# Turning the input of a streaming encoder: the RMS norm taken after the transpose instead of before it

## The chip, the cores and the metric

One core of a Trainium2 chip runs the whole program. The metric is device time in microseconds (us) of one execution. The engines are PE (TensorE, matrix products and transposes), DVE (VectorE), ACT (ScalarE), POOL (GpSimd) and SP (SyncE, which only issues DMAs here). All data are float32.

## The reference, cut to what matters

Two layers of a hybrid encoder are evaluated for 1024 prompt tokens and 32 sample tokens that share all weights. What matters here is the very first step, the RMS norm of the input of layer 0:

```python
def rms_norm(x, g):
    xf = x.astype(jnp.float32)
    y = xf * lax.rsqrt(jnp.mean(xf * xf, axis=-1, keepdims=True) + EPS)
    return (y * g.astype(jnp.float32)).astype(x.dtype)
...
        hp = rms_norm(yp, norm_g[l])
        hs = rms_norm(ys, norm_g[l])
```

`yp` is 1024 x 1024 and `ys` is 32 x 1024. Later the un-normed input is needed again for the residual sum.

## The kernel before

The program runs stage after stage, and each stage ends in a barrier of all engines: `turn_input`, then `gdn` (layer 0's delta-rule mixer), `band` (its chunk-band attention), `finish_layer` (output projection and memory attention), then `gla` and a second `finish_layer` for layer 1. The diff touches only the first stage, `turn_input`.

`turn_input` reads the input in 9 tiles of tokens: 8 tiles of 128 prompt tokens and a last one with the 32 sample tokens (`rows(t)`). In memory a token is a row of D = 1024 numbers; the later matrix products want features on the partitions. The stage makes two such turned copies, each with KD = 8 blocks of 128 features: `xT` (the raw input, a buffer called `x_kept` outside, which the trace shows under that name) and `hT` (the normed input times the gain `g`). Both are in SBUF, 128 partitions by 8 by 1152.

Each tile goes through the engines like this:

- SP issues one load per tile (L116), then the first four weight loads of the next stage (`load_ahead`, L59).
- ACT squares the tile with tokens on partitions and sums the squares on the way (L161, which makes a second small instruction that reads the accumulator), takes the logarithm (L163) and the exponential of minus half of it (L165). That is one number per token, `rs`, a column of 128 partitions by 1.
- DVE multiplies the tile by that column into `xN` (L193).
- PE turns the raw tile in 8 transposes of 128 x 128 into PSUM (`TX`, L139), and one tile behind turns `xN` in 8 transposes into `TH` (L126, `normed`).
- `TX` is copied to `xT` by ACT (L154, `turned`) for seven tiles and by DVE for tiles 2 and 5 (L198, `BY_DVE`).
- DVE multiplies `TH` by the gain into `hT` (L182, `out`).
- POOL only makes the identity (L172, L174) and is free after that.

Every buffer between engines has two halves, and each engine runs its own fixed list of instructions with semaphore waits. The next stage begins on PE with the products of L512 (`hT` and the weights `Wb`); its lists begin once every engine has passed the barrier.

Of the kernel before, what the change touches and what calls it, by code (L numbers as in the profile page):

```python
# [6 lines left out]
F32 = mybir.dt.float32  # L7
# [78 lines left out]
def turn_input(nc, ident, ones, eps, x_in, xT, gain, hT, ahead):  # L86

    with ExitStack() as ctx:
# [6 lines left out]
        xN = sb("xN", [128, 2, D])  # L95
        sq = sb("sq", [128, D])
        ss, rs = sb("ss", [128, TILES]), sb("rs", [128, TILES])
        g = sb("g", [128, KD])
        TX = ctx.enter_context(nc.psum_tensor("turn_TX", [128, 2, KD, 128], F32))
        TH = ctx.enter_context(nc.psum_tensor("turn_TH", [128, 2, KD, 128], F32))  # L100
        g_ld, x_ld = sem("g_ld"), [sem(f"x_ld{t}") for t in range(TILES)]
        cleared, ident_ok, consts = sem("cleared"), sem("ident_ok"), sem("consts")
        squared, rooted, rs_ok, scaled = sem("squared"), sem("rooted"), sem("rs_ok"), sem("scaled")
        x_turned, h_turned, x_act, x_dve, h_out = (sem("x_turned"), sem("h_turned"), sem("x_act"), sem("x_dve"), sem("h_out"))
        BY_DVE = (2, 5)
        by_dve = [len([t for t in BY_DVE if t < n]) for n in range(TILES + 1)]

# [3 lines left out]
        with nc.Block() as block:  # L111
# [8 lines left out]
            def _(pe):  # L120
                def normed(t):
                    r = rows(t)
                    pe.wait_ge(scaled, t + 1)
                    wait(pe, h_out, t - 1)
                    for k in range(KD):
                        mm = pe.transpose(TH[:, t % 2, k, 0:r], xN[0:r, t % 2, 128 * k:128 * k + 128], ident[0:r, 0:r])  # L126
                    mm.then_inc(h_turned, 1)

                pe.wait_ge(ident_ok, 1)
                for t in range(TILES):  # L130
                    r = rows(t)
                    pe.wait_ge(x_ld[t], 16)
                    if t >= 2:
                        if t - 2 in BY_DVE:
                            pe.wait_ge(x_dve, by_dve[t - 1])
                        else:
                            pe.wait_ge(x_act, t - 1 - by_dve[t - 1])
                    for k in range(KD):
                        mm = pe.transpose(TX[:, t % 2, k, 0:r], xS[0:r, t, 128 * k:128 * k + 128], ident[0:r, 0:r])  # L139
                    mm.then_inc(x_turned, 1)  # L140
                    if t:
                        normed(t - 1)
                normed(TILES - 1)

            @block.scalar
            def _(act):
# [3 lines left out]
                def turned(t):  # L150
                    if t in BY_DVE:
                        return
# [3032 lines left out]
```

## Time and profile before

| | us |
|---|---|
| median of 3 runs | 3585.02 (3584.09 to 3587.85) |
| the profiled execution, its own time | 3584.09 |
| its span in the trace | 3582.4 |
| PE busy over the span | 3484.0 (97%) |
| DVE, ACT, POOL busy | 1173.9, 1102.7, 512.4 |
| last instruction of `turn_input` ends | 26.63 after the span's start |
| first product of the next stage starts | 27.50 |

The span runs from the first to the last instruction in the trace. PE is the engine that is nearly always busy; a stage's end matters for the total when PE has nothing to do until the next stage starts.

### The profile page before, as it was taken

The page shows a single profiled execution, that of the slowest core. Times are in us where ns is not written, and L with a number is a line of the kernel's source. Part 1 is how long each engine was busy: PE and PEld are TensorE (multiplying, and loading weights), DVE is VectorE, ACT ScalarE, POOL GpSimd, SP SyncE. Part 2 cuts the span into 40 slices and gives each one's busy share as a digit, 9 for nine tenths or more (in the row PEclk, how much of TensorE's full clock was granted, in tenths as well). Part 3 has the DMA queues.
Part 4 walks back from the last instruction along what each step waited for, and adds up shares of the span by engine and source line. Part 5 has one row for each costly group of instructions (what it writes and reads, how often), then busy time and mean ns, then how long its engine had stood idle before and what let it go on. Part 6 is the DMA issues. An engine that isn't in the chain of part 4 may idle for free. (4 is left out here: it accounts for less than half of the span.)

```text
span 3582.4 us, 47127 instructions
## 1 busy us (share of the span) xinstructions
PE 3484.0 (97%) x16559; PEld 2563.4 (72%) x16559; DVE 1173.9 (33%) x2941; ACT 1102.7 (31%) x2810; POOL 512.4 (14%) x518
## 2 busy tenths in 40 slices
PE   9999999999799999999999998999999999899999
PEld 5777777776477778777766675677777777566676
DVE  3555555555133323333320233022222122220223
ACT  4343433333234333334210342122223222210242
POOL 2345543453000000000000002000000000011000
PEclk9999999999899999999999999999999999999999
DMA  6212411103322332212260102111111111371101
GB/s 161 52 32 38 37 36 27 37 24 116 72 40 42 46 41 43 42 29 92 92 213 30 36 24 74 36 30 45 39 50 44 44 30 33 117 232 48 35 1 49
DMA packets 246000, 206.64 MB, mean 58 GB/s; under 512 B 19903, under 2 KB 222943, under 8 KB 245831
## 3 DMA queue, kind: packets, MB, share of 16 engines
q1 hardware_dynamic: 239902, 194.16, 22.3%
q10 hardware_dynamic: 5936, 10.34, 0.8%
q8 instruction: 99, 1.62, 0.2%
q14 instruction: 63, 0.52, 0.0%
HBM read 158.49 MB, written 45.99 MB: 57 GB/s over the span
## 5 line engine op out<-in xcount | busy, mean ns | idle before, releaser
L512 PE MATMUL gdn_pj<-hT,Wb 128*128 128x352 f32 x1536 | 513.3, 460 | 1.6 <-PEq L45 1.6
L2014 PE MATMUL gla_pj<-hT,Wb 128*128 128x352 f32 x1536 | 471.7, 461 | 6.9 <-PEq L45 6.2
L1464 PE MATMUL band_pj<-hT,Wb 128*128 128x384 f32 (+1 forms) x1152 | 390.8, 468 | 25.4 <-PEq L45 14.4
L2014 PEld LDWEIGHTS gla_pj<-hT,Wb 128*128 128x128 f32 x1536 | 290.8, 190 | 157.2 <-issue 9.1
L512 PEld LDWEIGHTS gdn_pj<-hT,Wb 128*128 128x128 f32 x1536 | 264.8, 191 | 89.3 <-issue 1.7
L1464 PEld LDWEIGHTS band_pj<-hT,Wb 128*128 128x128 f32 x1152 | 208.8, 194 | 110.1 <-issue 30.9
L2010 PE MATMUL gla_pj<-gla_Wv,hT 128*128 128x256 f32 (+1 forms) x1152 | 266.8, 381 | 0.0
L2010 PEld LDWEIGHTS gla_pj<-gla_Wv,hT 128*128 128x128 f32 x1152 | 217.2, 190 | 31.8
L1649 ACT ACTIVATE band_E<-band_NS,band_nm 128x576 f32<-128x576 f32 (+9 forms) x136 | 89.8, 660 | 215.8 <-DVE band_nm L1727 215.4
L1226 POOL TENSOR_TENSOR x_kept<-gdn_AT,gdn_level 128x384 f32<-128x384 f32 x144 | 144.3, 1033 | 35.7 <-DVE gdn_TT L1008 18.5
L1494 PE MATMUL band_pj<-Wb,hT 128*128 128x128 f32 x1152 | 144.2, 275 | 0.0
L1557 PEld LDWEIGHTS band_PX<-band_ET,band_VT 128*128 128x128 f32 x976 | 127.0, 192 | 20.3
L1494 PEld LDWEIGHTS band_pj<-Wb,hT 128*128 128x128 f32 x1152 | 136.5, 192 | 0.7
L1727 DVE CUSTOM_DVE_ANT_0 band_NS<-band_SC,band_bias 128x576 f32<-128x576 f32 (+9 forms) x136 | 83.2, 612 | 153.1 <-issue 152.2
L1557 PE MATMUL band_PX<-band_ET,band_VT 128*128 128x128 f32 x976 | 131.0, 275 | 0.0
L2729 PE MATMUL fin_ps<-fin_R,fin_Wx 128*128 128x384 f32 (+1 forms) x384 | 124.7, 468 | 2.2 <-DVE fin_xT L3020 2.1
L2720 PE MATMUL fin_ps<-hT,Wb 128*128 128x384 f32 (+1 forms) x384 | 125.9, 463 | 0.0
L1659 ACT ACTIVATE band_ET<-band_PT 128x512 f32<-128x512 f32 (+3 forms) x136 | 70.7, 520 | 158.3 <-PE band_PX L1537 89.6
L1527 PE MATMUL band_SC<-band_KN,band_Qz 128*128 128x288 f32 (+3 forms) x448 | 115.8, 375 | 3.6 <-issue 3.6
L2693 PE MATMUL fin_ps<-hT,fin_Wq 128*128 128x384 f32 (+1 forms) x384 | 117.2, 459 | 0.0
L2661 PE MATMUL fin_ps<-hT,Wb 128*128 128x384 f32 (+1 forms) x384 | 115.9, 459 | 0.0
L2983 DVE TENSOR_TENSOR fin_xT<-fin_xT,fin_ps 128x384 f32<-128x384 f32 (+1 forms) x48 | 24.7, 520 | 274.4 <-PE fin_ps L2661 241.7
(413 smaller groups left out, 5375.4 us busy)
## 6 DMA issues: line engine op xcount, KB each, us to landing
Wb<-in_l_w_in_dram SPq DMA_DIRECT2D x96, 512.0 KB, 6.6
fin_xT<-x_features SPq DMA_DIRECT2D x16, 528.0 KB, 7.6
fin_R<-o_features SPq DMA_DIRECT2D x16, 528.0 KB, 9.4
Wb<-in_l_w_mkv_dram SPq DMA_DIRECT2D x8, 1024.0 KB, 5.4
Wb<-in_l_w_out_dram SPq DMA_DIRECT2D x16, 512.0 KB, 3.7
gla_Wv<-in_l_w_in_dram SPq DMA_DIRECT2D x8, 1024.0 KB, 5.5
o_features<-gla_OF ACTq DMA_DIRECT2D x14, 528.0 KB, 5.7
gdn_GB<-gate_rows SPq DMA_DIRECT2D x8, 544.0 KB, 3.6
```

What stands on the lines that cost most here:

```text
L512: mm = pe.matmul(pj[:, m % 2, 0:w], W[:, j, k, :], hT[:, k, c0:c0 + w], start=k == 0, stop=k == KD - 1)
L1226: pool.tensor_tensor(g3(BT, g), g3(AT, g), mask, ALU.mult).then_inc(masked, 1)
L1464: mm = pe.matmul(out[:, 0:w], W[:, BAND_SLOT[j], k, :], hT[:, k, c0:c0 + w], start=k == 0, stop=k == KD - 1)
L1494: mm = pe.matmul(out[:, 0:128], hT[:, k, 128 * i:128 * i + 128], W[:, BAND_SLOT[3], k, :], start=k == 0, stop=k == KD - 1)
L1527: mm = pe.matmul(out[:, b, 0:w], q, KN[p][:, k0 + w * b:k0 + w * b + w], start=True, stop=True)
L1557: mm = pe.matmul(PX[:, 1, :], v, ET[:, u % 2, 128 * b:128 * b + 128], start=b == 0, stop=b == blocks(u) - 1)
L2010: mm = pe.matmul(pj[:, m % 2, 0:wv], hT[:, k, 128 * x:128 * x + 128], Wv[:, k, 0:wv], start=k == 0, stop=k == KD - 1)
L2014: mm = pe.matmul(pj[:, m % 2, 0:w], W[:, SLOT[kind], k, :], hT[:, k, c0:c0 + w], start=k == 0, stop=k == KD - 1)
L2661: mm = pe.matmul(ps[:, 3 * (n % 2) + c, 0:w], weights, src[:, c0:c0 + w], start=i == 0, stop=i == len(tiles) - 1)
L2693: mm = pe.matmul(ps[:, i % 3, 0:w], Wqt[:, h, k, :], hT[:, k, c0:c0 + w], start=k == 0, stop=k == KD - 1)
L2720: mm = pe.matmul(out[:, 0:w], Wz[:, x, k, :], hT[:, k, c0:c0 + w], start=k == 0, stop=k == KD - 1)
L2729: mm = pe.matmul(out[:, 0:w], Wo[:, k, 128 * x:128 * x + 128], O[:, k, c0:c0 + w], start=k == 0, stop=k == M_H - 1)
```

## The change

The norm is now taken with features on the partitions. Only the raw tile is turned (`TP`, two halves, L139 now), and ACT copies every tile to `xT`. POOL squares the turned tile from `xT` into `sq`. PE sums the squares over all 1024 features by 8 products with a 128 x 128 matrix of ones, so that every partition of `PS` holds the sums of all tokens of the tile. ACT takes logarithm and exponential of that, now 128 partitions by 128 tokens instead of one column. DVE multiplies `xT` by the gain (a column) and by `rs` (a full tile) in 8 instructions per tile, one per block of features, into `hT`. The transposes of `xN`, the scaling into `xN`, DVE's two copies and ACT's squares are gone.

```diff
             def _(pe):
+                def total(t):
+                    pe.wait_ge(squared, t + 1)
+                    wait(pe, rooted, t - 1)
                     for k in range(KD):
-                        mm = pe.transpose(TH[:, t % 2, k, 0:r], xN[0:r, t % 2, 128 * k:128 * k + 128], ident[0:r, 0:r])
-                    mm.then_inc(h_turned, 1)
+                        mm = pe.matmul(PS[:, t % 2, 0:rows(t)], ones[:, :], sq[:, t % 2, k, 0:rows(t)], start=k == 0, stop=k == KD - 1)
+                    mm.then_inc(summed, 1)
...
                 for t in range(TILES):
                     r = rows(t)
                     pe.wait_ge(x_ld[t], 16)
+                    wait(pe, copied, t - 1)
                     for k in range(KD):
+                        mm = pe.transpose(TP[:, t % 2, k, 0:r], xS[0:r, t, 128 * k:128 * k + 128], ident[0:r, 0:r])
+                    mm.then_inc(turned, 1)
                     if t:
+                        total(t - 1)
+                total(TILES - 1)
...
             def _(act):
+                def root(t):
+                    r = rows(t)
+                    act.wait_ge(summed, t + 1)
+                    wait(act, h_out, t - 1)
+                    act.activation(rs[:, t % 2, 0:r], PS[:, t % 2, 0:r], ACT.Ln, scale=1.0 / D, bias=eps[:, 0:1]).then_inc(rooted, 1)
+                    act.wait_ge(rooted, t + 1)
+                    act.activation(rs[:, t % 2, 0:r], rs[:, t % 2, 0:r], ACT.Exp, scale=-0.5).then_inc(rs_ok, 1)
...
                 for t in range(TILES):
                     r = rows(t)
-                    act.activation(sq[0:r, :], xS[0:r, t, :], ACT.Square, accum_out=ss[0:r, t:t + 1]).then_inc(squared, 1)
+                    act.wait_ge(turned, t + 1)
+                    act.activation(xT[:, :, cols(t)], TP[:, t % 2, :, 0:r], ACT.Copy).then_inc(copied, 1)
                     if t:
+                        root(t - 1)
+                root(TILES - 1)
...
             def _(pool):
+                for t in range(TILES):
+                    pool.wait_ge(copied, t + 1)
+                    wait(pool, summed, t - 1)
+                    pool.tensor_tensor(sq[:, t % 2, :, 0:rows(t)], xT[:, :, cols(t)], xT[:, :, cols(t)], ALU.mult).then_inc(squared, 1)
...
             def _(dve):
                 for t in range(TILES):
                     r = rows(t)
+                    dve.wait_ge(copied, t + 1)
                     dve.wait_ge(rs_ok, t + 1)
-                    dve.tensor_scalar(xN[0:r, t % 2, :], xS[0:r, t, :], rs[0:r, t:t + 1], None, ALU.mult).then_inc(scaled, 1)
+                    for k in range(KD):
+                        mm = dve.scalar_tensor_tensor(hT[:, k, cols(t)], xT[:, k, cols(t)], g[:, k:k + 1], rs[:, t % 2, 0:r],
+                                                      ALU.mult, ALU.mult)
+                    mm.then_inc(h_out, 1)
```

In the helper `wait`, a wait for a count of zero or less is left out. So ACT may start the root of tile t once tiles 0 to t-2 are in `hT`, and PE may turn tile t once tiles 0 to t-2 are copied.

## Rows read from the trace of the kernel before

**Rows 1.** The page's first part: busy time, share and instructions per engine.

```profile
PE 3484.0 (97%) x16559; PEld 2563.4 (72%) x16559; DVE 1173.9 (33%) x2941; ACT 1102.7 (31%) x2810; POOL 512.4 (14%) x518
```

**Rows 2.** Windows: stretch, length, then busy us (count) per engine, granted clock, DMA share, GB/s.

```profile
0.00:26.63 26.63, 18.67 (x144) 16.57 (x144) 19.07 (x23) 21.05 (x44) 0.70 (x6) 1.00 0.96 218
27.50:60.00 32.50, 32.50 (x127) 16.45 (x128) 0.96 (x4) 6.18 (x9) 8.28 (x32) 1.00 0.81 220
```

**Rows 3.** Timeline of PE in `turn_input`: start, length, line, shape, count, idle before.

```profile
4.88 4.04 PE L139 MATMUL turn_TX<-ident,turn_xS 128*128 128x128 f32 x16 [4.88 <-DMA turn_xS<-in_x_prompt_dram]
...
10.60 1.04 PE L126 MATMUL turn_TH<-ident,turn_xN 128*128 128x128 f32 x8
...
27.50 14.44 PE L512 MATMUL gdn_pj<-hT,Wb 128*128 128x352 f32 x48 [1.60 <-PEq L45]
```

**Rows 4.** Timeline of DVE at the end of `turn_input`.

```profile
23.20 1.22 DVE L182 TENSOR_TENSOR hT<-turn_TH,turn_g 128x1024 f32<-128x1024 f32 x1
24.42 0.74 DVE L193 TENSOR_SCALAR turn_xN<-turn_xS,turn_rs 32x1024 f32<-32x1024 f32 x1
25.09 1.54 DVE L182 TENSOR_TENSOR hT<-turn_TH,turn_g 128x1024 f32<-128x1024 f32 x2
```

**Rows 5.** Timeline of ACT: one tile in `turn_input`.

```profile
16.08 1.05 ACT L161 ACTIVATE turn_sq<-turn_xS 128x1024 f32<-128x1024 f32 x1
...
17.68 1.01 ACT L154 ACTIVATE x_kept<-turn_TX 128x1024 f32<-128x1024 f32 x1
```

**Rows 6.** Groups by line and shape, ACT: busy us, mean ns of one, idle before.

```profile
L2843 ACT ACTIVATE fin_rs<-fin_ps,eps 128x384 f32<-128x384 f32 x4 | 2.2, 562 | 0.0
L845 ACT ACTIVATE x_kept<-x_kept 128x128 f32<-128x128 f32 x64 | 19.1, 298 | 0.1
```

**Rows 7.** Groups by line and shape, POOL.

```profile
L1191 POOL TENSOR_TENSOR gdn_conv<-gdn_conv,gdn_tap 128x1091 f32<-128x1091 f32 x24 | 50.7, 2113 | 1.9
L3088 POOL TENSOR_TENSOR fin_acc<-fin_acc,fin_sq 128x384 f32<-128x384 f32 x28 | 27.9, 996 | 462.6 <-ACT fin_sq L2837 462.6
L1211 POOL TENSOR_TENSOR gdn_WQ<-gdn_act,gdn_EG 128x384 f32<-128x384 f32 x24 | 23.4, 1003 | 0.0
L3088 POOL TENSOR_TENSOR fin_acc<-fin_acc,fin_sq 128x288 f32<-128x288 f32 x14 | 11.1, 794 | 65.1 <-ACT fin_sq L2837 65.0
L2361 POOL COPY gla_Ss<-gla_sall 128x256 f32 x6 | 2.3, 390 | 0.0
```

**Rows 8.** Groups by line and shape, DVE.

```profile
L2966 DVE SCALAR_TENSOR_TENSOR hT<-fin_xT,fin_g,fin_rs 128x384 f32<-128x384 f32 x32 | 17.3, 613 | 6.6 <-ACT fin_rs L2845 6.6
L1706 DVE SCALAR_TENSOR_TENSOR band_Qz<-band_raw,band_g,band_rs 64x32 f32<-64x32 f32 x16 | 3.9, 245 | 0.0
```

**Rows 9.** Timeline of DVE: nine instructions of 128 columns without a pause.

```profile
100.66 2.45 DVE L937 SCALAR_TENSOR_TENSOR x_kept<-gdn_GB,gdn_gn,gdn_causal 128x128 f32<-128x128 f32 x9
```

**Rows 10.** Timeline, 123.50 to 126.2 us: DVE and POOL beside each other.

```profile
123.50 0.55 DVE L1008 TENSOR_TENSOR gdn_TT<-ident,x_kept 128x384 f32<-128x384 f32 x1
...
123.72 1.19 POOL L1226 TENSOR_TENSOR x_kept<-gdn_AT,gdn_level 128x384 f32<-128x384 f32 x1 [2.49 <-DVE gdn_TT L1008]
123.97 1.36 DVE L1008 TENSOR_TENSOR gdn_TT<-ident,x_kept 128x384 f32<-128x384 f32 x1
...
124.87 1.31 POOL L1226 TENSOR_TENSOR x_kept<-gdn_AT,gdn_level 128x384 f32<-128x384 f32 x1
```

**Rows 11.** Timeline, 214.5 to 217.2 us: DVE and POOL beside each other.

```profile
214.59 1.84 DVE L977 SCALAR_TENSOR_TENSOR gdn_conv<-gdn_U,gdn_cwc,gdn_conv 128x1091 f32<-128x1091 f32 x1
...
214.46 0.83 POOL L1206 TENSOR_TENSOR x_kept<-x_kept,gdn_cur 128x384 f32<-128x384 f32 x1 [11.18 <-ACT x_kept L799]
...
215.61 1.51 POOL L1206 TENSOR_TENSOR x_kept<-x_kept,gdn_cur 128x384 f32<-128x384 f32 x1 [0.33 <-ACT x_kept L799]
```

**Rows 12.** One line of the kernel each: shortest, median, longest ns, first and last start.

```profile
L977 DVE SCALAR_TENSOR_TENSOR gdn_conv<-gdn_U,gdn_cwc,gdn_conv x48: 1354/1356/1845, 104.6 to 816.5; 128x1091 f32<-128x1091 f32 x48
L1021 DVE TENSOR_TENSOR gdn_TT<-gdn_TT,gdn_X x120: 514/517/555, 129.5 to 859.8; 128x384 f32<-128x384 f32 x120
```

More of the change, by code:

```diff
@@ L94, in turn_input @@
         xS = sb("xS", [128, TILES, D])
-        xN = sb("xN", [128, 2, D])
-        sq = sb("sq", [128, D])
-        ss, rs = sb("ss", [128, TILES]), sb("rs", [128, TILES])
+        sq = sb("sq", [128, 2, KD, 128])
+        rs = sb("rs", [128, 2, 128])
         g = sb("g", [128, KD])
-        TX = ctx.enter_context(nc.psum_tensor("turn_TX", [128, 2, KD, 128], F32))
-        TH = ctx.enter_context(nc.psum_tensor("turn_TH", [128, 2, KD, 128], F32))
+        TP = ctx.enter_context(nc.psum_tensor("turn_TP", [128, 2, KD, 128], F32))
+        PS = ctx.enter_context(nc.psum_tensor("turn_PS", [128, 2, 512], F32))
         g_ld, x_ld = sem("g_ld"), [sem(f"x_ld{t}") for t in range(TILES)]
         cleared, ident_ok, consts = sem("cleared"), sem("ident_ok"), sem("consts")
[L103 to L106, printed above, removed]
+        turned, copied, squared, summed, rooted, rs_ok, h_out = (sem("turned"), sem("copied"), sem("squared"), sem("summed"),
+                                                                 sem("rooted"), sem("rs_ok"), sem("h_out"))
         def cols(t):
@@ L148, in _ @@
                 act.preload_act_table_set("natural_log_exp_and_others")
-                def turned(t):
-                    if t in BY_DVE:
-                        return
-                    act.wait_ge(x_turned, t + 1)
-                    act.activation(xT[:, :, cols(t)], TX[:, t % 2, :, 0:rows(t)], ACT.Copy).then_inc(x_act, 1)
+                def root(t):
[5 more added lines that the diff above has]
+                    act.activation(rs[:, t % 2, 0:r], rs[:, t % 2, 0:r], ACT.Exp, scale=-0.5).then_inc(rs_ok, 1)
                 act.wait_ge(consts, 1)
@@ L158, in _ @@
                     r = rows(t)
-                    act.wait_ge(x_ld[t], 16)
-                    wait(act, squared, t)
-                    act.activation(sq[0:r, :], xS[0:r, t, :], ACT.Square, accum_out=ss[0:r, t:t + 1]).then_inc(squared, 1)
-                    act.wait_ge(squared, t + 1)
-                    act.activation(rs[0:r, t:t + 1], ss[0:r, t:t + 1], ACT.Ln, scale=1.0 / D, bias=eps[0:r, 0:1]).then_inc(rooted, 1)
-                    act.wait_ge(rooted, t + 1)
-                    act.activation(rs[0:r, t:t + 1], rs[0:r, t:t + 1], ACT.Exp, scale=-0.5).then_inc(rs_ok, 1)
+                    act.wait_ge(turned, t + 1)
+                    act.activation(xT[:, :, cols(t)], TP[:, t % 2, :, 0:r], ACT.Copy).then_inc(copied, 1)
                     if t:
-                        turned(t - 1)
-                turned(TILES - 1)
+                        root(t - 1)
+                root(TILES - 1)
             @block.gpsimd
```

28 lines of the change are left out of this document (2 added, 26 removed).

## The prediction

> **What bounds the kernel now.** I read the page's engine shares first, then windows of the first stage and of the stretch behind it, then the timelines of PE, DVE and ACT in the stage, and last the groups and timelines that price what the change adds. PE is busy 97% of the span [rows 1]. In the first 26.63 us it is busy for only 18.67 us, and from 27.50 on it is busy without a gap, at a granted clock of 1.00 [rows 2]. So the stage's end sets the total: whatever the stage grows or shrinks by, the rest of the program is pushed or pulled by, since every engine waits at the barrier between 26.63 and 27.50 [rows 3, 4]. An earlier or later start changes nothing in what follows it, as no wait on a DMA shows on PE there that could take up a delay. Inside the stage no engine is full: ACT needs 16.08 to 18.69, 2.61 us, for a tile that it also copies [rows 5], PE needs 1.04 us for a group of 8 transposes, twice a tile [rows 3], and DVE's last gain product ends the stage at 25.09 + 1.54 = 26.63 [rows 4].
>
> **What the change takes and gives, part by part.**
>
> ACT loses the square, its accumulator read and two tiny instructions. It gains a logarithm and an exponential of 128 columns. The nearest rows are 0.562 us for a logarithm of 384 columns out of PSUM and 0.298 us for 128 columns out of SBUF [rows 6]; the larger shape less 256 columns at about 0.8 ns (0.298 us for 128 against 1.01 for the 1024 of a copy, over 896 [rows 5, 6]) gives some 0.36. With 0.31 for the exponential, the root costs 0.67, call it 0.7 with the semaphore between. A tile then costs ACT 0.7 + 1.01 = 1.7 us instead of 2.6. This saving is real, but ACT's time is no longer what the stage waits for.
>
> PE swaps 8 transposes for 8 products with the same 128 columns: 1.04 us each way [rows 3], call it 1.1 until the result is seen. No gain. The first 16 transposes took 4.04 us where 8 later ones take 1.04, so the first two tiles will again take 2.0 each.
>
> DVE loses per tile a scale of 0.74 and a gain product of 1.22 us [rows 4], and the two copies. It gains 8 instructions of 128 columns with two SBUF inputs. The same form ran nine times in 2.45 us, 0.26 apart [rows 9]; the same operation into `hT` at 384 columns takes 0.613 [rows 8]. Eight cost 7 x 0.26 + 0.35 = 2.2 us. So DVE is slower per tile, 2.2 against 1.96 us. The last tile of 32 columns pays 8 times nearly the same fixed cost: 0.245 each [rows 8], about 0.16 apart if they overlap as the long ones do, 1.4 us.
>
> POOL gains a product of 128 x 1024 per tile. No row has this size. Two tensor inputs cost 0.996 us for 384 columns and 0.794 for 288, so 2.1 ns a column, and in three pieces of 128 it is 1.003 [rows 7]: 0.996 + 640 x 0.0021 = 2.35, and 2.4 with the eight pieces. From below, 2.113 us for 1091 columns in one piece gives 2.0; from above, 8/3 of 1.003 gives 2.7. I take 2.4, because the operands lie in pieces as in the 1.003 row. The last tile, 256 columns, costs 0.75.
>
> The DVE and POOL parts cannot be laid side by side. At 123.97 a DVE product with two SBUF inputs took 1.36 us where the one before took 0.55: it ended only after POOL's product, which had begun at 123.72. POOL's next one took 1.31 instead of 1.00 behind it [rows 10, 7]. The form that the change uses (tensor, column, tensor, all in SBUF) did the same: 1.84 us beside POOL against a median of 1.356, and POOL's product then took 1.51 against 0.83 [rows 11, 12]. A DVE product with one input in PSUM keeps to 514 to 555 ns over 120 times, with POOL busy beside many of them [rows 12]. So a two-SBUF-input instruction of DVE and a product of POOL take turns, one whole instruction each. Before the change POOL had nothing to do in this stage, and now every DVE instruction of it meets one.
>
> The Trainium skill (SBUF — State Buffer, "Who interferes with whom") states the rule that speaks against this change: a DVE instruction with two SBUF inputs shares its second read interface with GpSimd, and whichever issues first blocks the other for a whole instruction. The rows above agree, and by it the sum below stands; by its absence the sum would be that of the second case.
>
> **The sum.** Tile 0 is turned at 4.88 + 2.0 = 6.9, copied at 7.9, squared at 10.3, summed at 11.4, its root ready at 12.1. PE's list has the sums of tile 0 ahead of turning tile 2, so that is turned at 12.4 and copied at 13.4. POOL squares tile 1 until 12.7 and tile 2 from 13.4 to 15.8; DVE gets in three instructions before and one between; tile 3 is copied at 15.8 and squared until about 18.5; DVE's other four put tile 0 into `hT` at about 19.6. From there ACT's two-deep wait makes a loop: `hT` of tile t, then the root of t+2 (0.7), the copy of t+4 (1.0), its square on POOL (2.4, after the DVE instruction then running, 0.1), then what is left of DVE's eight for tile t+1, of which six or seven ran during root and copy (0.3 to 0.4). That is 4.5 us a tile, which is also the sum of the two engines' work, 2.2 + 2.4, less a little. Four turns bring tile 4 to 19.6 + 18.0 = 37.6. POOL's big squares are then done. Tiles 5, 6, 7 take 2.2 each plus 0.8 for POOL's last small square, and tile 8 takes 1.4: 7.4 + 1.4 = 8.8, end at 46.4. Against 26.63 this is +19.8 us. The profiled execution has 3584.1, which is 0.9 under the median of the runs shown; 3585.0 + 19.8 = 3604.8, and as some 0.1 us of each recorded duration seems not to block the other (the DVE instruction at 123.97 ended at 125.33, where 124.91 + 0.55 would be 125.46 [rows 10]), I take 3604.
>
> Bounds inside this case: POOL at 2.0 makes the loop 4.1 and the end 43.5 (3602), at 2.7 it makes 4.8 to 4.9 and the end 49 (3608). DVE's 0.26 might be 0.23 or 0.30: two us either way.
>
> **The rivals.**
>
> Second case, no collision worth the name: DVE and POOL run side by side. Then two tiles go round in transposes 1.0 + copy 1.0 + square 2.4 + sums 1.1 = 5.5 us, because PE and ACT each take the turned tile t+2 only after the sums and root of t. Turned tiles 2, 4, 6, 8 at 12.4, 17.9, 23.4, 28.6; the last root at 31.6, DVE done with tile 7 at 33.3 and tile 8 at 34.7. That is +8.1: 3593, with POOL at 2.0 3591 and at 2.7 3595. Rows 10 and 11 speak against it; for it speaks only that 128-column instructions are shorter than those seen to collide.
>
> Third case, on the other side, not slower: POOL's price. If a product of a tensor with itself costs POOL what a one-input copy does, 0.390 for 256 columns [rows 7], some 1.0 for 1024, and it slips between DVE's instructions, DVE is the bound. Its first instruction can start at 6.9 + 1.0 + 1.0 + 1.1 + 0.7 = 10.7, and 8 x 2.2 + 1.4 = 19.0 more end at 29.7: +3, 3588, within 0.2%. It needs a square under about 1.7 us; all two-tensor rows say over 2.0. Even this is not faster than before, because DVE's work alone, begun at 10.7, ends later than 26.63 unless its instructions come under 0.22 us apart.
>
> Fourth case, the clock: PE would be busy about 2.1 of each 4.5 us. A group of 8 took 2.0 us at the start of the trace and 1.04 later [rows 3], which is what half the clock would do. In the loop PE's groups are not on the path (tile t+4 is turned while DVE works), so the price is one group at the end, 1 us, and the first products of the next stage: they come 48 in 14.44 us, 0.3 each [rows 3], and ten of them at half the clock would lose 3 us. 3604 + 4 = 3608.
>
> The Trainium skill (TensorE: Matmul & The Clock Gate, "HAM oscillation — how this bites in real kernels") says that waits between short groups of products can throw PE back to its lower clock. The trace grants 1.00 through this stage before the change, with PE busy 70% of it, and no row of this stage shows the fall.
>
> **How the numbers follow.** Taking turns as summed: 0.70. With the lower clock on top: 0.07. No collision: 0.14. The cheap square: 0.05. The remaining 0.04 is for anything else, a gain included. The range 3593 to 3609 holds the first two and part of the second case; the likeliest case's own range is 3600 to 3608. A change under 0.2%, 7.2 us, is about what a measurement of this kernel can't tell from none. The second case straddles that line, two parts in three above it. Slower by more than 0.2%: 0.70 + 0.07 + 0.09 + 0.01 = 0.87. Within: 0.05 + 0.05 + 0.01 = 0.11. Faster: 0.02.
>
> **What would show it.** The stage's last DVE instruction ends near 46, and PE starts the next stage 0.9 us later. POOL's squares last 2.4 us, a little more where they wait for DVE, with gaps of some 2 us between them from tile 4 on. DVE's instructions are mostly 0.35 long, but one or two in each eight last over 2 us, each over one of POOL's. If instead none of DVE's is over 0.5 us, the second case holds. Copies of tiles 4 to 7 on ACT start 4.5 us apart. Everything from the barrier on is as before, only later. The prediction is wrong if POOL squares in under 1.7 us, if DVE's short instructions slip through, or if something behind the barrier takes the delay back.

## The result, and the profile after

The change makes the kernel slower: 3609.3 us (median of 4 runs, 3608.6 to 3609.8) against 3586.4 (4 runs, 3584.1 to 3590.2), a ratio of 1.0063, 95% interval 1.0048 to 1.0079. That is 22.9 us more, where 17.6 were forecast (3604 less the 3586.4 of these runs) and 3609 was the upper end of the range. The profiled execution took 3610.3 us, 26.2 more than that of before.

The page's first part after the change, to be laid beside [rows 1]:

```profile
PE 3499.8 (97%) x16631; PEld 2577.4 (71%) x16631; DVE 1178.3 (33%) x2993; ACT 1095.7 (30%) x2794; POOL 533.1 (15%) x527
```

PE has 72 more instructions and is busy for 15.8 us more; DVE has 52 more. Both counts turn out to matter. So does a line of the page's third part: packets, MB and share of the queue q14, whose kind the profile gives as `instruction`, before and after.

```profile
q14 instruction: 63, 0.52, 0.0%
q14 instruction: 87, 0.71, 0.1%
```

Windows of the kernel after (columns as in [rows 2]): the whole stage, the first 48 products of the next, and three stretches chosen for the clock column, third from the end.

```profile
0.00:48.31 48.31, 33.54 (x216) 31.65 (x216) 26.14 (x75) 15.56 (x28) 21.25 (x15) 0.89 0.62 134
49.17:66.58 17.41, 17.41 (x49) 10.61 (x50) 0.62 (x3) 2.37 (x4) 7.90 (x30) 0.83 0.69 209
30.00:35.00 5.00, 0.00 (x0) 0.00 (x0) 3.69 (x15) 1.20 (x2) 5.00 (x1) 0.97 0.16 40
35.00:40.00 5.00, 4.51 (x24) 4.28 (x24) 0.00 (x0) 0.65 (x2) 2.29 (x2) 0.50 0.00 0
50.60:52.00 1.40, 1.40 (x4) 0.88 (x3) 0.00 (x0) 0.00 (x0) 1.36 (x7) 0.50 0.23 14
```

The stage ends at 48.31 instead of 26.63. The timeline of DVE, its rows in the stage from the first product on; the last line is one instruction out of the first row:

```profile
14.45 19.24 DVE L182 SCALAR_TENSOR_TENSOR hT<-x_kept,turn_g,turn_rs 128x128 f32<-128x128 f32 x48 [12.54 <-ACT turn_rs L149]
40.13 2.55 DVE L182 SCALAR_TENSOR_TENSOR hT<-x_kept,turn_g,turn_rs 128x128 f32<-128x128 f32 x8 [6.44 <-ACT turn_rs L149]
44.83 3.49 DVE L182 SCALAR_TENSOR_TENSOR hT<-x_kept,turn_g,turn_rs 128x128 f32<-128x128 f32 x16 [2.15 <-ACT turn_rs L149]
...
22.20 1.98 DVE L182 SCALAR_TENSOR_TENSOR hT<-x_kept,turn_g,turn_rs 128x128 f32<-128x128 f32 x1
```

The timeline of POOL, the squares of tiles 4, 5 and 6:

```profile
21.98 2.05 POOL L169 TENSOR_TENSOR turn_sq<-x_kept 128x1024 f32<-128x1024 f32 x1 [1.43 <-ACT x_kept L155]
24.67 2.05 POOL L169 TENSOR_TENSOR turn_sq<-x_kept 128x1024 f32<-128x1024 f32 x1 [0.64 <-ACT x_kept L155]
29.18 6.26 POOL L169 TENSOR_TENSOR turn_sq<-x_kept 128x1024 f32<-128x1024 f32 x1 [2.47 <-ACT x_kept L155]
```

Laid over each other, these rows show two kinds of waiting. POOL's square of tile 4 began at 21.98, and the DVE instruction issued at 22.20 took 1.98 us instead of 0.34, ending 0.15 behind the square. The same happened beside the squares at 15.95, 18.61 and 24.67. At 29.18 it went the other way: DVE was inside a row of products without a pause (48 from 14.45 to 33.69), and POOL's square lasted 6.26 us where the others take 1.89 to 2.05. It ended 1.75 us behind DVE's row, so it did its work only when that row was over, some 4.4 us late.

The timeline of PE: the first group of transposes, the first sums (of tile 0), later sums, and the groups around that square:

```profile
4.67 1.94 PE L132 MATMUL turn_TP<-ident,turn_xS 128*128 128x128 f32 x8 [4.67 <-DMA turn_xS<-in_x_prompt_dram]
...
9.77 3.79 PE L122 MATMUL turn_PS<-turn_sq,ones 128*128 128x128 f32 x16 [0.69 <-POOL turn_sq L169]
...
17.92 2.05 PE L122 MATMUL turn_PS<-turn_sq,ones 128*128 128x128 f32 x16 [0.45 <-POOL turn_sq L169]
...
28.66 1.04 PE L132 MATMUL turn_TP<-ident,turn_xS 128*128 128x128 f32 x8
35.49 3.78 PE L122 MATMUL turn_PS<-turn_sq,ones 128*128 128x128 f32 x16 [5.80 <-POOL turn_sq L169]
...
49.17 17.41 PE L497 MATMUL gdn_pj<-hT,Wb 128*128 128x352 f32 x48 [2.97 <-PEq L45]
66.51 14.53 PE L682 MATMUL gdn_P<-hT,gdn_wab 128*40 128x512 f32 x48
```

The 8 products of a sum are recorded as 16 passes and take 2.05 us (the row at 17.92), against 1.04 for 8 transposes. PE sat idle for 5.80 us before the sums of tile 6, which then took 3.78: the granted clock was 0.97 while it waited and 0.50, the lower level of 1.2 GHz, from 35 on (windows above). The next stage starts at 49.17 against 27.50 [rows 3], 21.7 late, and its first 48 products take 17.41 us instead of 14.44: the clock is 0.50 again at 50.60. At 66.51 PE is 24.6 us late.

Behind that the delay does not stay what it is. Start of the same PE work, after less before, from the two timelines (an "end" is the last product of L512 for `gdn` and of L1464 for `band`, after the change L497 and L1449):

| work | us late |
|---|---|
| first products of the stage `gdn` | 21.7 |
| `gdn_P` (66.51 against 41.87) | 24.6 |
| end of `gdn` (843.8 against 807.1) | 36.7 |
| start of `band` | 35.8 |
| end of `band` (1710.2 against 1686.5) | 23.7 |
| `gla` | 22.3 |
| last `fin`, its second group of products | 27.9 |
| end of the span | 26.2 |

The list of waits after the change has two rows that are not in that of before (waiting engine and tile, what it waited for, total us, times, longest):

```profile
DVE gdn_cwc L937 <- issue: 12.9, 5, 2.7
DVE gdn_cz L943 <- issue: 8.9, 5, 2.0
```

and that of before has one that is not in the one of after:

```profile
PE band_pj L1464 <- issue: 8.0, 2, 5.8
```

### The profile page after: what moved, and what is told of

It is laid out like the page before. It is cut to its first block and busy times, and to the rows that moved or that the text cites. A ratio compares the mean times of both kernels' runs of the same rounds, so it can differ in the third digit from the quotient of the medians.

```text
span 3608.6 us, 47321 instructions
## 1 busy us (share of the span) xinstructions
PE 3499.8 (97%) x16631; PEld 2577.4 (71%) x16631; DVE 1178.3 (33%) x2993; ACT 1095.7 (30%) x2794; POOL 533.1 (15%) x527
## 3 DMA queue, kind: packets, MB, share of 16 engines
q8 instruction: 100, 1.64, 0.2%
## 5 line engine op out<-in xcount | busy, mean ns | idle before, releaser
L497 PE MATMUL gdn_pj<-hT,Wb 128*128 128x352 f32 x1536 | 516.3, 462 | 3.0 <-PEq L45 3.0
L1449 PE MATMUL band_pj<-hT,Wb 128*128 128x384 f32 (+1 forms) x1152 | 387.1, 465 | 16.8 <-PEq L45 13.8
L497 PEld LDWEIGHTS gdn_pj<-hT,Wb 128*128 128x128 f32 x1536 | 266.3, 192 | 92.1 <-issue 5.5
L1449 PEld LDWEIGHTS band_pj<-hT,Wb 128*128 128x128 f32 x1152 | 207.2, 192 | 99.7 <-issue 19.5
L1995 PEld LDWEIGHTS gla_pj<-gla_Wv,hT 128*128 128x128 f32 x1152 | 217.2, 190 | 31.8
L1211 POOL TENSOR_TENSOR x_kept<-gdn_AT,gdn_level 128x384 f32<-128x384 f32 x144 | 144.2, 1032 | 35.8 <-DVE gdn_TT L993 18.5
L2705 PE MATMUL fin_ps<-hT,Wb 128*128 128x384 f32 (+1 forms) x384 | 124.8, 460 | 0.0
L3073 POOL TENSOR_TENSOR fin_acc<-fin_acc,fin_sq 128x384 f32<-128x384 f32 (+1 forms) x42 | 39.0, 929 | 532.2 <-ACT fin_sq L2822 532.0
L2354 POOL TENSOR_TENSOR gla_OR<-gla_OR,gla_rs 128x768 f32<-128x768 f32 x24 | 35.3, 1469 | 552.4 <-ACT gla_rs L2196 552.4
```

The costliest lines, as they stand in the source:

```text
L497: mm = pe.matmul(pj[:, m % 2, 0:w], W[:, j, k, :], hT[:, k, c0:c0 + w], start=k == 0, stop=k == KD - 1)
L1211: pool.tensor_tensor(g3(BT, g), g3(AT, g), mask, ALU.mult).then_inc(masked, 1)
L1449: mm = pe.matmul(out[:, 0:w], W[:, BAND_SLOT[j], k, :], hT[:, k, c0:c0 + w], start=k == 0, stop=k == KD - 1)
L1995: mm = pe.matmul(pj[:, m % 2, 0:wv], hT[:, k, 128 * x:128 * x + 128], Wv[:, k, 0:wv], start=k == 0, stop=k == KD - 1)
L2705: mm = pe.matmul(out[:, 0:w], Wz[:, x, k, :], hT[:, k, c0:c0 + w], start=k == 0, stop=k == KD - 1)
```

## The experiments

All times are medians against runs of the kernel before on the same chip (medians 3587.3 to 3587.6). "Late" is the start of the first `gdn` products less 27.50.

**e1: no shared read.** The change with the root in PSUM, so that DVE's product reads one SBUF tensor only.

```diff
-        rs = sb("rs", [128, 2, 128])
+        rs = ctx.enter_context(nc.psum_tensor("turn_rs", [128, 2, 512], F32))
```

> The changed kernel with one edit: the tile rs that ACT writes and DVE reads lies in PSUM instead of SBUF. All arithmetic is as in the changed kernel. Theory (DVE and POOL take turns because DVE's instructions have two SBUF inputs): now no DVE instruction lasts over 0.5 us, where nine lasted 0.7 to 2 us, and no square of POOL lasts over 2.0 us, where one lasted 6.26. The loop of turning 1.04, copying 1.02, squaring 1.9 and summing 1.95 us then sets the pace, 6.0 us for two tiles, PE never idles for 5 us, its clock stays up, and the stage ends near 38 instead of 48.3; the next stage's first 48 products take 14.4 us again. Total 11 to 13 us over the kernel before, 3597 to 3599. Rival (the two engines only look coupled, the waits come from the semaphores or from any SBUF traffic): DVE's long instructions and the end near 48 stay, total 3609.

3601.2 us (5 runs), ratio 1.0037 (1.0023 to 1.0051): 8 us less than the change. DVE ends the stage at 39.10 instead of 48.31, late 12.5. One line each of e1's kernel (shortest, median, longest ns):

```profile
L182 DVE SCALAR_TENSOR_TENSOR hT<-x_kept,turn_g,turn_rs x72: 242/342/349, 14.3 to 38.9; 128x128 f32<-128x128 f32 x64, 128x32 f32<-128x32 f32 x8
L169 POOL TENSOR_TENSOR turn_sq<-x_kept x9: 613/1892/1893, 7.8 to 33.4; 128x1024 f32<-128x1024 f32 x8, 128x256 f32<-128x256 f32 x1
```

and the same line of the change:

```profile
L182 DVE SCALAR_TENSOR_TENSOR hT<-x_kept,turn_g,turn_rs x72: 244/340/1984, 14.4 to 48.1; 128x128 f32<-128x128 f32 x64, 128x32 f32<-128x32 f32 x8
```

The median is the same, the longest fell from 1984 ns to 349, and no square lasts over 1893. One operand moved out of SBUF removes both kinds of waiting, so they hang on DVE's second SBUF input and not on the semaphores. That is worth 9.2 us at the stage's end, and 3.9 of these are the clock's, as e2 shows. What is left, 12.5 us late with no collision at all, is the second case of the prediction, which had put its end at 34.7.

**e2: PE kept busy.** The change with 48 transposes of the identity between the turning of tile 7 and the sums of tile 6, where PE had been idle.

```diff
+                    if t == 7:
+                        for _ in range(48):
+                            pe.transpose(PJ[:, 0:128], ident[:, :], ident[:, :])
                     if t:
                         total(t - 1)
```

> The changed kernel with one addition: after turning tile 7 PE does 48 more transposes of the identity into a spare PSUM bank, some 5.3 us of work in a stretch where it idled 5.8 us. Theory (a granted clock of 0.50 from about 35 to 54 us cost 4 us in the stage and 3 us in the 48 products behind the barrier): the clock stays at 1.00, the sums of tile 6 take 1.95 instead of 3.8 us, the stage ends near 44.4 instead of 48.3, the first 48 products of the next stage take 14.4 instead of 17.4, total about 7 us less than the changed kernel, 3602. POOL's square of 6.26 us stays. Rival (the clock did not matter, DVE or POOL set the end): the end stays within 1 us of 48.3.

PE's timeline in e2:

```profile
29.18 5.40 PE L137 MATMUL turn_PJ<-ident 128*128 128x128 f32 x48
35.40 2.05 PE L123 MATMUL turn_PS<-turn_sq,ones 128*128 128x128 f32 x16 [0.82 <-POOL turn_sq L173]
```

POOL's square still lasts 6.26, but the sums behind it take 2.05 instead of 3.78, and DVE ends at 44.38 instead of 48.31. So of the stage's growth 3.9 us came from the clock, and its fall inside the stage from PE's idle time. At the barrier it falls again (3.48 us idle, first 48 products 17.18). The kernel's time did not follow the stage: 3611.6 us (4 runs), ratio 1.0065 (1.0048 to 1.0082). Its `band` takes back only 6.3 us where that of the change takes back 12.1: a wait of PE for nothing that the profile shows is back there, of 5.0 us. The table below comes to that.

**e3: DVE lets POOL go first.** The change with DVE's products of tile 4 waiting until tile 6 is squared.

```diff
                     dve.wait_ge(rs_ok, t + 1)
+                    if t == 4:
+                        dve.wait_ge(squared, 7)
```

> The changed kernel with one wait more: DVE starts tile 4 only when POOL has squared tile 6. Theory (POOL's square of tile 6, ready at 29.18, got no turn until DVE's unbroken row of instructions ended at 33.7, and PE's idle time and slower clock come from that): the square of tile 6 takes under 2.3 us and ends near 31.2 instead of 35.4, the clock stays at 1.00, the stage ends near 44 or earlier, total 7 to 10 us under the changed kernel, 3599 to 3602. Rival (the square was long for another reason): it still takes over 5 us. Second rival (the total of both engines' work sets the end whatever the order): the end moves by less than 1 us.

POOL's timeline in e3:

```profile
22.53 5.30 POOL L169 TENSOR_TENSOR turn_sq<-x_kept 128x1024 f32<-128x1024 f32 x2 [1.91 <-ACT x_kept L155]
30.05 1.89 POOL L169 TENSOR_TENSOR turn_sq<-x_kept 128x1024 f32<-128x1024 f32 x1 [2.22 <-ACT x_kept L155]
...
37.06 5.62 POOL L169 TENSOR_TENSOR turn_sq<-x_kept 128x256 f32<-128x256 f32 x1 [2.35 <-ACT x_kept L155]
```

The square of tile 6, at 30.05, is down to 1.89. But that of tile 4 now takes 3.40 of the first row's 5.30: it was kept out for 1.5 us and then got in at 24.1, between two instructions of a row of DVE that went on. And the small last one, 0.71 us in the change, takes 5.62: POOL is kept out for 4.9 us there instead. DVE's row around it ends at 42.21, 0.47 before the square:

```profile
32.08 10.13 DVE L184 SCALAR_TENSOR_TENSOR hT<-x_kept,turn_g,turn_rs 128x128 f32<-128x128 f32 x32 [2.52 <-POOL turn_sq L169]
```

The stage is as late as ever (21.8), and the time is 3609.2 us (4 runs), ratio 1.0057 (1.0041 to 1.0074). The long square is thus no property of tile 6; any square that meets a long row of DVE can be kept out.

**e4: another phase.** A memset of 128 x 64 (0.15 us) on POOL ahead of the square of tile 6, so that it asks at another point of DVE's row.

```diff
+                    if t == 6:
+                        pool.memset(late[:, :], 0.0)
                     pool.tensor_tensor(sq[:, t % 2, :, 0:rows(t)], xT[:, :, cols(t)], xT[:, :, cols(t)], ALU.mult).then_inc(squared, 1)
```

> The changed kernel with one addition: POOL clears a spare 128 x 64 tile, 0.14 us, between its waits and the square of tile 6, so that the square asks for its turn 0.1 to 0.2 us later within DVE's beat of 0.26 us. Of POOL's squares that began within a row of DVE's, those that began 0.04 to 0.18 us after a DVE instruction got the next turn, and the one that began 0.03 us after lost it for 4.4 us. Theory A (the phase decides): the square of tile 6 now gets the next turn, takes 2.0 to 2.3 us, the clock stays up and the total falls by 7 to 10 us. Theory B (a long row of DVE instructions keeps POOL out, whatever the phase): the square still waits until the row ends and the total stays at 3609.

The first of the two squares in POOL's row at 28.94 again lasts 6.17 us:

```profile
28.84 0.15 POOL L171 MEMSET turn_late<- 128x64 f32 x1 [2.71 <-ACT x_kept L156]
28.94 8.02 POOL L172 TENSOR_TENSOR turn_sq<-x_kept 128x1024 f32<-128x1024 f32 x2
```

3607.6 us (4 runs), ratio 1.0058 (1.0041 to 1.0074), late 21.3. It asked 0.24 us earlier, 0.12 us behind the start of a DVE instruction where that of the change asked 0.03 behind one, and was kept out all the same. Squares that got in at once asked 0.02 to 0.18 us behind one in these two kernels, so an unlucky moment is not the cause.

**e5: no collision and no fall of the clock.** e1 with 26 transposes of the identity behind PE's last sums.

```diff
                 total(TILES - 1)
+                pe.wait_ge(copied, TILES)
+                for _ in range(26):
+                    pe.transpose(TP[:, 0, 0, :], ident[:, :], ident[:, :])
```

> The kernel with rs in PSUM, and after its last sums PE does 26 transposes of the identity into the PSUM that the last copy has freed, some 3 us of work while DVE finishes. In the run with rs in PSUM the granted clock was 0.87 over 35 to 40 us and 0.50 over the next 5, and the first 48 products of the next stage took some 17.1 us instead of 14.44. Theory (the clock fell because PE had next to nothing to do while DVE finished): the clock stays at 1.00 through the barrier and the 48 products take 14.4 to 14.8 us; the stage ends at 39.1 as before, total 2.7 us less than with rs in PSUM alone. Rival (the barrier itself, 1 us without work, lets the clock fall, or the products are slow for another reason): the 48 products stay near 17 us.

PE's timeline in e5:

```profile
35.67 3.04 PE L139 MATMUL turn_TP<-ident 128*128 128x128 f32 x26
39.54 14.44 PE L500 MATMUL gdn_pj<-hT,Wb 128*128 128x352 f32 x48 [0.83 <-PEq L45]
```

The first 48 products take 14.44 us, as before the change, instead of e1's 17.20: 2.8 us of e1's delay were the clock behind the barrier. 3594.8 us (10 runs), ratio 1.0022 (1.0013 to 1.0032). That is 6.4 less than e1; 2.4 more of it come from `band` (table below).

**e6: half the sums.** e1 with the sums over four of the eight blocks.

```diff
-                    for k in range(KD):
+                    for k in range(4):
```

> The kernel with rs in PSUM, with the sums of squares taken over 4 of the 8 blocks of features only (the other 4 are left out). Theory (without collisions two tiles go round in one loop of transposes 1.04, copy 1.02, square 1.89 and sums 1.95 us, so each us of the sums counts once for two tiles): the sums of a tile take 1.0 us, the loop falls from 6.0 to 5.05 us, and the stage ends some 4.5 us earlier, near 34.6. Rival (POOL or DVE sets the pace by itself, their work per tile being 1.89 and 2.2): the end moves by less than 1 us.

DVE ends the stage at 34.42, 4.7 us before e1 does. The loop of two tiles (turning, copy, square, sums) is what sets the stage once the collisions are gone, and PE's sums are on it. The single run took 3609.3 us, though the next stage starts 4.6 us earlier than in e1. Its page counts 16559 instructions of PE, 72 fewer than e1's, and its `band` does not take back the 12 us that e1's does: PE's waits for nothing shown are there as in the kernel before, 7.9 us against 8.0. This was the sign that something behind the stage reacts to the lists of instructions.

**e7: gaps in DVE's row.** The change with a one-column memset behind each of DVE's products but every eighth, 63 in all.

```diff
+                        if k < KD - 1:
+                            dve.memset(gap[:, KD * t + k:KD * t + k + 1], 0.0)
```

> The changed kernel, with DVE clearing one spare column, some 0.06 us without an SBUF input, between the eight instructions of each tile. Theory (POOL is kept out for up to 4.4 us because DVE's row of two-input instructions leaves no gap): each square of POOL gets its turn at the next gap, none lasts over 2.4 us, PE's idle stretch before the sums of tile 6 is gone or under 3 us, and the stage ends at 44 or earlier although DVE has 0.4 us more work per tile. Rival (who gets the turn does not depend on a gap): at least one square still lasts over 3 us.

One line of e7's kernel:

```profile
L170 POOL TENSOR_TENSOR turn_sq<-x_kept x9: 675/1892/1954, 7.9 to 34.9; 128x1024 f32<-128x1024 f32 x8, 128x256 f32<-128x256 f32 x1
```

No square is over 1.95 us, and the stage ends at 42.0 although DVE has 63 instructions more. The one run took 3587.2 us, as fast as the kernel before (3587.5). But the stage is still 15.4 late; the rest was given back elsewhere, and two things had been changed: the gaps and the count.

**e10: the same count, no gaps.** The same 63 memsets in a block ahead of DVE's loop.

```diff
+                for i in range(63):
+                    dve.memset(pad[:, i:i + 1], 0.0)
                 dve.wait_ge(g_ld, 16)
```

> The changed kernel, with 63 clears of a spare column on DVE ahead of the loop, as many as the run with gaps had between its instructions. If the gaps did their work as gaps, the long square of POOL (over 4 us), the idle PE and the end near 48 are back. If the list's length did what remained, DVE's waits in gdn's heads (12.9 and 8.9 us over five heads in the changed kernel) are gone, PE is 24 to 25 us late through all of gdn instead of 36.7 at its end, and the total is near 3597, 12 us under the changed kernel. Rival: the waits in gdn stay and the total is 3609.

POOL's timeline in e10, squares of tiles 6 and 7:

```profile
29.23 8.11 POOL L170 TENSOR_TENSOR turn_sq<-x_kept 128x1024 f32<-128x1024 f32 x2 [2.47 <-ACT x_kept L156]
```

Those 8.11 us for two squares are what the change has too, and the stage ends at 48.35: in e7 it was the gaps that let POOL in. But the time is 3596.1 us (10 runs), ratio 1.0023 (1.0014 to 1.0033), 13 us less than the change, with a stage that is no faster. The count alone gives that.

**e8, e9, e12: the kernel before with padding.** e8 adds 52 one-column memsets to DVE, e9 adds 72 transposes of 32 x 32 to PE, both ahead of the stage's loop, where those engines wait for the first tile; e12 has the 72 and 115 memsets.

```diff
+                for i in range(52):
+                    dve.memset(pad[:, i:i + 1], 0.0)
```
```diff
+                for _ in range(72):
+                    pe.transpose(TX[0:32, 0, 0, 0:32], ident[0:32, 0:32], ident[0:32, 0:32])
```

> The kernel before, with 52 clears of a spare column added on DVE in turn_input while DVE has nothing else to do, so that DVE's list is as much longer as the change made it. Theory (behind the stage the two kernels differ by how their instruction lists lie, not by work: in the changed kernel DVE waits 2.6 us for nothing the profile shows in five heads of gdn and PE runs 12 us later after them, and it runs 12 us earlier again in band): the stage ends at 26.6 us as before, but DVE's waits in gdn's heads appear, and PE is 5 to 12 us later at the end of gdn. Rival (those waits come from the later start of gdn or from what its loads meet): gdn runs as in the kernel before, total within 1.5 us of it.

> The kernel before, with 72 transposes of a 32 x 32 corner of the identity on PE ahead of the first tile, in time in which PE waits for its first load, so that PE's list is as much longer as the change made it. Theory (behind the stage only the place of the instructions in memory differs): the stage ends within 1.5 us of 26.63, gdn runs as before, and PE's two waits in band for which the profile shows no cause, 8.0 us in the kernel before, are gone, so that PE is 8 to 14 us earlier at the end of band and the total is some 8 to 12 us under the kernel before, 3576 to 3580. Rival (band was faster in the changed kernels because it started later, against its loads): total within 2 us of the kernel before.

> The kernel before, with both paddings: 72 small transposes on PE and 115 clears of a spare column on DVE, which is DVE's list at the length of the run with gaps. Theory: the stage ends near 26.6 to 28, no DVE waits in gdn, none of PE's in band, total 8 to 12 us under the kernel before and within 2 us of the run with PE's padding alone, so 3575 to 3580: the shortest of all. Rival: the two paddings disturb each other and the total is at or over the kernel before.

e8: 3598.9 us (9 runs), ratio 1.0033 (1.0022 to 1.0043). e9: 3576.7 (6 runs), 0.9969 (0.9957 to 0.9982). e12: 3575.7 (6 runs), 0.9965 (0.9953 to 0.9977). The stage itself is 0.3, 0.1 and 0.6 late. In e9 and e12 the clock fell behind the barrier all the same: the first 48 products take 16.13 and 15.92 us, with a granted clock of 0.79 and 0.62 from 27 to 30, though PE was idle for 1.6 us there as in the kernel before, where it stayed at 1.00. So the idle time just before the products is not all that decides. e8 has the waits that the change brought, in its own list of waits:

```profile
DVE gdn_cwc L955 <- issue: 12.9, 5, 2.7
DVE gdn_cz L961 <- issue: 8.4, 5, 1.8
PE band_pj L1467 <- issue: 7.7, 1, 7.7
```

The third row is the one of before, and it is missing in e9 and e12. So 52 instructions that do nothing reproduce the change's loss in `gdn`, and 72 others most of its gain in `band` (10.8 of 12.1 us).

**e11: all of it.** e5 with the 63 memsets ahead of the loop.

```diff
+        rs = ctx.enter_context(nc.psum_tensor("turn_rs", [128, 2, 512], F32))
...
+                for _ in range(26):
+                    pe.transpose(TP[:, 0, 0, :], ident[:, :], ident[:, :])
...
+                for i in range(63):
+                    dve.memset(pad[:, i:i + 1], 0.0)
```

> The kernel with rs in PSUM and PE kept busy until the barrier, with the same 63 clears on DVE. Theory: gdn starts 12 us later than in the kernel before and its heads keep that, without DVE's waits; band gives back 12 to 15 us as in the other kernels with the longer PE list; the total is 3583 to 3586, at or a little under the kernel before, from a stage that is 12 us longer. Rival (DVE's waits in gdn come with any later start): total stays at 3595.

3583.1 us (11 runs), ratio 0.9990 (0.9981 to 0.9999), with the stage 12.0 late: 0.1% below the kernel before, hardly told from nothing, and 7.4 us above e12, which has the old stage and the same count on DVE. The changed stage does not pay in any form that was tried.

**The count, over all kernels.** The counts of DVE and PE are from each page's first part; they are of recorded instructions, a product counting twice, a transpose once and a wait for a semaphore not at all. "In `gdn`" is by how much the delay against before grows from `gdn_P` to the end of `gdn`, "in `band`" from the start of `band` to its end, in us.

| kernel | DVE | in `gdn` | PE | in `band` |
|---|---|---|---|---|
| before | 2941 | 0 | 16559 | 0 |
| e9 | 2941 | 0.0 | 16631 | -10.8 |
| e8 | 2993 | +11.5 | 16559 | -3.3 |
| e6 | 2993 | +11.8 | 16559 | -0.4 |
| the change | 2993 | +12.1 | 16631 | -12.1 |
| e1 | 2993 | +11.8 | 16631 | -12.4 |
| e3 | 2993 | +11.8 | 16631 | -12.5 |
| e4 | 2993 | +11.1 | 16631 | -12.3 |
| e5 | 2993 | +11.9 | 16657 | -14.8 |
| e2 | 2993 | +11.6 | 16679 | -6.3 |
| e7 | 3056 | -0.1 | 16631 | -15.1 |
| e10 | 3056 | -0.1 | 16631 | -14.8 |
| e11 | 3056 | -0.1 | 16657 | -14.6 |
| e12 | 3056 | -0.1 | 16631 | -11.4 |

What `gdn` loses goes with DVE's count and with nothing else in the table: 11.1 to 12.1 us in all eight kernels with 2993, 0.1 or less in all with another count. The queue q14 goes with it: 87 or 88 packets and 0.71 or 0.72 MB on the pages of those eight, 63 or 64 packets and 0.52 MB on the pages of the other six. What `band` gives back goes with PE's waits for nothing shown at `band_pj`: 7.7 to 8.0 us of them in the three kernels with 16559, 5.0 in e2, none in the others.

## Why the prediction was wrong in its size

**The step that failed.** "In the loop PE's groups are not on the path", with the lower clock left to a fourth case of 0.07, was the term that put the time outside the range: the clock took 6.9 us by `gdn_P`. Behind it stands a step of the mechanism: "take turns, one whole instruction each", with a square going ahead "after the DVE instruction then running, 0.1". One square waited 4.4 us instead, PE stood idle for it, and the clock fell. Against the 19.8 that were forecast for the profiled run, the stage without the clock's share grew by 17.8 (it would end at 44.4, as e2's does), the clock added 6.9, and the rest of the program, where 12.1 more and 12.1 less cancel, 1.5: 26.2. That the stage's own end came within 1.9 us is luck: it was forecast 2.0 too late and lost 3.9 to the clock.

**What held.** The stage's end sets the time up to the barrier; the change is slower; a DVE instruction with two SBUF inputs and a square of POOL block each other, and e1 shows that this costs 9.2 us at the stage's end with what the clock adds to it. The two-tile loop is what remains without it. The next stage starts 0.86 us behind the last DVE instruction, as forecast.

**The likeliest case's end, 46.4 forecast, 48.31 measured.** The sum came near by terms that missed in both directions.

- POOL's square was taken at 2.4 and measures 1.89 (2.05 with a DVE instruction beside it). No price for operands "in pieces" shows; even the bound from below, 2.0, was too high. All its rows were of two different tensors or of other shapes.
- PE's sums, "8 products with the same 128 columns: 1.04 us each way", measure 1.95 to 2.05. A product is recorded as two passes, a transpose as one. "No gain" was a loss of 0.9 us a tile. This term is on the loop of the second case: 34.7 forecast, 39.1 measured in e1. Two tiles go round in 1.0 + 1.0 + 1.9 + 2.0 and the waits between. e1's copies of tiles 4, 5, 6 and 7 start at 21.14, 23.80, 27.15 and 29.81, so 6.0 us for two where 5.5 were forecast; and at the start one group of sums takes 3.79 us in the change, where 1.1 was in the sum. That is what a group takes at a granted clock of 0.50 (3.78), though the clock column has 1.00 there, as it has for the first transposes of 1.94.
- The loop of 4.5 us a tile, from strict turns, did not come about. Copies of tiles 3 to 7 start 3.4, 2.7, 4.5 and 2.1 us apart, and only four of DVE's instructions met a square, at 1.64 us each. The fifth time POOL was kept out for 4.4 us. "Take turns, one whole instruction each" and "after the DVE instruction then running, 0.1" is the step of the mechanism that failed: POOL does not always get in behind the instruction then running. It may be kept out while many go by, up to the end of DVE's row. e3, e4, e7 and e10 show that the row is what does it: in e3 it moves to other squares that meet one, a shift of 0.24 us doesn't cure it, small gaps in the row do, and the same instructions ahead of the row don't. The gap instructions are one-column memsets; whether it is the pause or their other kind of access that lets POOL in was not separated. Nor is it settled what decided for the four other squares, which met the same row of 48 and got in at once, or for that of e3 which got in after 1.5 us without a pause in the row.

The Trainium skill (SBUF — State Buffer, "Who interferes with whom") has the pair as an exclusive lock that whoever issues first holds for a whole instruction. The four DVE instructions of 1.98 us agree. The square of 6.26 us does not: POOL asked at 29.18, ahead of at least 16 of DVE's instructions, and all of them went first. The measurement decides.

**The clock.** The fourth case was given 0.07 and 4 us (1 in the stage, 3 behind it). It came about, and at 6.9: 3.9 in the stage, which e2 gives back, and 3.0 behind the barrier, which e5 does not have. "In the loop PE's groups are not on the path" failed because the stall of POOL was not foreseen: the sums of tiles 6 to 8 stood at the end of the only path there was, at half the clock. Two rows had pointed to it: the groups of twice the length at the start, and a forecast PE that is busy 2.1 of 4.5 us. The 3 us behind the barrier were priced right, and should have stood in the likeliest case: e1 loses 2.8 there without any stall of POOL. That sum would be 46.4 + 1 + 3, 3608.

The Trainium skill (TensorE: Matmul & The Clock Gate, "HAM oscillation — how this bites in real kernels") says that waits between products can send PE to its lower clock. The trace of the change agrees: 5.80 us idle, then 0.50.

**"Everything from the barrier on is as before, only later."** This failed by the largest terms, though they nearly cancel. `gdn` grows by 12.1 us and `band` shrinks by 12.1. The first is shown to come from DVE's count of 2993 (e8: the old kernel plus 52 idle memsets gives +11.5; e7 and e10: 3056 takes it away). It shows as DVE's "issue" waits of 2.6 and 1.8 us at five heads of `gdn`, of which this is one of the change, from DVE's timeline:

```profile
329.96 0.18 DVE L937 COPY gdn_cwc<-gdn_taps 128x21 f32 x1 [2.57 <-issue]
...
332.33 0.17 DVE L943 COPY gdn_cz<-gdn_tok 64x9 f32 x1 [1.82 <-issue]
```

Nothing was late for that copy: the engine waited for nothing that the page names. The trace has the rest. `gdn` runs its inner heads in a loop (`dve.Fori(1, H_A - 1)`), and DVE's branch back to the loop's start is recorded at 326.86. A packet of 8192 bytes on q14, the queue of kind `instruction`, starts at 327.92, the first copy of the next head at 329.96; another packet at 330.36, the next copy at 332.33. It is so at all five jumps back: one packet in each of the ten waits. The kernel before jumps back too (302.27 the first time), has no packet on q14 between 295 and 823 us, and no such wait; e10 has none between 323 and 852. So the ten waits are read as waits for instructions that are loaded again at each turn of the loop. A turn takes 102.8 us instead of 100.4, five times, which is the 12.1. Why a list of 2993 needs that and one of 2941 or 3056 doesn't, no run shows.

The second goes with PE's list. The kernel before has such a gap of its own, from PE's timeline:

```profile
1308.55 0.49 PE L1464 MATMUL band_pj<-hT,Wb 128*128 128x384 f32 x1
...
1314.81 2.29 PE L1464 MATMUL band_pj<-hT,Wb 128*128 128x384 f32 x3 [5.77 <-issue]
```

With 72 instructions ahead of it this is gone (e9). It and one more of 2.3 us, each 9 to 11 us behind a jump back of `band`'s loop, are 8.0 of the 12.1 us that `band` gains; in e2, with 16679 instructions, one of 5.0 is back, which is most of what its `band` lacks. Where the other 4 us come from stays open.

Nearly all of the 5.6 us that the last `fin` loses are at its first group of products, here before and after, from PE's timelines:

```profile
3171.42 28.64 PE L2645 MATMUL fin_ps<-hT,Wb 128*128 128x384 f32 x96 [2.64 <-PEq L45]
3196.42 31.53 PE L2630 MATMUL fin_ps<-hT,Wb 128*128 128x384 f32 x96 [5.04 <-PEq L45]
```

PE waits 2.4 us longer at the barrier, and the group then takes 2.9 more, at a granted clock of 0.50 over its first 4.6 us where the kernel before has 1.00: the loss behind the first barrier once more. Why that barrier opens later stays open.

**The sum of the profiled run, as measured:** 21.7 (of it 3.9 clock) + 3.0 clock behind the barrier + 12.1 `gdn` - 0.9 between - 12.1 `band` - 1.4 up to `gla` + 5.6 to the last `fin` - 1.7 to the end = +26.3, against 26.2 from the two spans. Forecast were 19.8 + 0 + 0. Had the padding effects been absent, the delay would be about the 24.6 at `gdn_P`: 3584.1 + 24.6 = 3608.7, still at the upper edge of the range.

**The best version.** e12 and e9 beat the kernel before by 0.3%. They compute in the old way, and their gain comes from the length of the list, not from the change. It holds for this program as it stands, and any edit can move it again.

## What to carry to other kernels

Before work is moved to GpSimd, list which DVE instructions of that stretch read two SBUF tensors: each can be blocked for a whole GpSimd instruction, and a long row of them can keep GpSimd out for 4 to 5 us; one operand in PSUM removes both. When PE is to wait in a stage, price its next groups and the first products behind the barrier at the lower clock in the likeliest case, not in a rival. And when a change of 0.3% is judged, repeat the kernel before with as many idle instructions as the change adds to each engine: here 52 memsets alone made 12 us. Look at the queues of kind `instruction` on the page and at "issue" waits behind a loop's turn.

## What the runs showed of the hardware

- A square of 128 x 1024 on GpSimd, one tensor times itself, takes 1.89 us; two different tensors of 1091 columns took 2.11 [rows 7].
- Eight float products of 128 columns take 1.95 to 2.05 us on PE and are recorded as 16 passes; eight transposes of the same size take 1.04.
- A GpSimd instruction that had been issued waited 4.4 us (and 4.9 in e3) while DVE instructions that start 0.26 us apart went ahead of it.
- The count of instructions ahead in an engine's list changed the time of stages hundreds of us later by 12 us, in either direction, with nothing but "issue" in the list of waits. In `gdn` each such wait of DVE (1.7 to 2.7 us) follows a loop's jump back and has one 8192-byte packet of the queue q14, kind `instruction`, in it.
